# Sharing out a depthwise convolution anew, and beginning it during the projection ahead of it

## What is computed

```python
def conformer_conv(h, pw1_w, pw1_b, dw_w, dw_b, ln_g, ln_b, pw2_w, pw2_b):
    a = h @ pw1_w + pw1_b                      # first pointwise projection, 1024 -> 2048
    u, g = jnp.split(a, 2, axis=-1)
    u = u * jax.nn.sigmoid(g)
    u = lax.conv_general_dilated(u, dw_w[:, None, :], window_strides=(1,),
        padding=[(CONV_PAD, CONV_PAD)], dimension_numbers=("NWC", "WIO", "NWC"),
        feature_group_count=D_MODEL) + dw_b    # depthwise, 31 taps
    mu = jnp.mean(u, axis=-1, keepdims=True)
    var = jnp.mean(jnp.square(u - mu), axis=-1, keepdims=True)
    u = ((u - mu) * lax.rsqrt(var + NORM_EPS)) * ln_g + ln_b
    return jax.nn.silu(u) @ pw2_w + pw2_b      # second pointwise projection
```

## Time and profile before

| What | Value |
|---|---|
| Median of 3 runs | 3033.05 us (3025.01 to 3033.93) |
| The profiled execution's span, first to last instruction | 3031.5 us |
| Mean granted TensorE clock, as a share of full speed | 0.930 |
| TensorE matmul busy | 2768.4 us (91%) |
| VectorE busy | 1539.5 us (51%) |
| ScalarE busy | 1286.9 us (42%) |
| GpSimd busy | 142.2 us (5%) |

### The profile page before, as it was taken

The page is one execution under the profiler, slowest core; times in us unless marked ns, Lnnn a source line. Parts: engine busy times, 40 slices in busy tenths (PEclk is TensorE's granted clock), DMA queues, the critical chain, the costliest instruction groups (busy, mean ns, idle before and its releaser), DMA issues. The chain is left out here.

```text
span 3031.5 us, 41708 instructions
## 1 busy us (share of the span) xinstructions
PE 2768.4 (91%) x15680; PEld 2291.4 (76%) x15680; DVE 1539.5 (51%) x2209; ACT 1286.9 (42%) x1896; POOL 142.2 (5%) x114
## 2 busy tenths in 40 slices
PE   5999998995899999899998798997999988888997
PEld 3778786843678778678876658997769987867997
DVE  4544424397644433544323565546645456465554
ACT  4544422333444432444312354544435545354543
POOL 0000000750000000000000000000000001000000
PEclk9999999998999999999999899998869999679998
DMA  6344442200344433344322202543314444302543
GB/s 233 139 152 163 173 151 82 92 19 1 111 152 166 153 111 111 125 149 156 126 96 97 98 1 108 183 178 141 111 42 159 169 160 154 125 1 83 181 166 128
DMA packets 52713, 374.70 MB, mean 124 GB/s; under 512 B 5823, under 2 KB 7035, under 8 KB 8737
## 3 DMA queue, kind: packets, MB, share of 16 engines
q1 hardware_dynamic: 50144, 358.63, 33.0%
q0 software_dynamic: 1920, 12.27, 1.2%
q10 hardware_dynamic: 576, 2.83, 0.3%
HBM read 372.55 MB, written 7.39 MB: 125 GB/s over the span
## 5 line engine op out<-in xcount | busy, mean ns | idle before, releaser
L968 DVE TENSOR_TENSOR wlo<-raw,whi 128x1024 fp32r<-128x1024 f32 x682 | 823.0, 1229 | 921.7 <-ACT whi L631 921.3
L631 ACT ACTIVATE whi<-raw 128x1024 fp32r<-128x1024 f32 x682 | 701.0, 1053 | 923.9 <-PE acc L1378 855.7
L1376 PE MATMUL acc<-hhi,whi 128*128 128x256 f32 (+1 forms) x2768 | 933.5, 337 | 70.0 <-DVE hlo L1033 40.2
L1377 PE MATMUL acc<-hlo,whi 128*128 128x256 f32 (+1 forms) x2768 | 928.4, 335 | 0.0
L1378 PE MATMUL acc<-hhi,wlo 128*128 128x256 f32 (+1 forms) x2768 | 927.2, 335 | 0.0
L1376 PEld LDWEIGHTS acc<-hhi,whi 128*128 128x128 f32 x2768 | 535.0, 193 | 131.2 <-issue 78.6
L1378 PEld LDWEIGHTS acc<-hhi,wlo 128*128 128x128 f32 x2768 | 534.9, 193 | 50.8
L1377 PEld LDWEIGHTS acc<-hlo,whi 128*128 128x128 f32 x2768 | 535.2, 193 | 48.4 <-issue 0.2
L1376 PE MATMUL acc<-ghi,whi 128*128 128x512 f32 (+1 forms) x1056 | 363.4, 344 | 21.7 <-DVE glo L1079 21.7
L1377 PE MATMUL acc<-glo,whi 128*128 128x512 f32 (+1 forms) x1056 | 361.4, 342 | 0.0
L1378 PE MATMUL acc<-ghi,wlo 128*128 128x512 f32 (+1 forms) x1056 | 360.5, 341 | 0.0
(11 more groups left out here) (222 smaller groups left out, 2671.9 us busy)
## 6 DMA issues: line engine op xcount, KB each, us to landing
raw<-in_slabs SPq DMA_DIRECT2D x341, 1024.0 KB, 4.8
skew_dram<-lines_dram POOLq DMA_DIRECT2D x1, 6144.0 KB, 23.6
bt<-skew_dram POOLq DMA_DIRECT2D x4, 1024.0 KB, 6.9
x<-in_x_in ACTq DMA_DIRECT2D x1, 2048.0 KB, 8.1
out<-x SPq DMA_DIRECT2D x1, 1024.0 KB, 4.8
rope<-in_rope POOLq DMA_DIRECT2D x1, 512.0 KB, 4.7
mask<-in_mask POOLq DMA_DIRECT2D x1, 512.0 KB, 5.3
ptok<-in_p POOLq DMA_DIRECT2D x2, 256.0 KB, 5.2
```

Source lines behind the costliest of these rows:

```text
L631: nc.scalar.activation(whi[:, n % 2, cols], raw[:, n % 2, cols], ACT.Copy).then_inc(ready, 1)
L968: nc.vector.tensor_tensor(wlo[:, n % 2, cols], raw[:, n % 2, cols], whi[:, n % 2, cols].bitcast(F32), ALU.subtract).then_inc(low, 1)
L1376: nc.tensor.matmul(out, w[0], xx[0], start=first, stop=False)
L1377: nc.tensor.matmul(out, w[0], xx[1], start=False, stop=False)
```

## The change

The convolution's tiles are shared out as 0 and 1 (VectorE, early), 2 and 3 (GpSimd), 4 and 5 (VectorE, late), 6 and 7 (TensorE).
- Tap 0 with the bias is now made by ScalarE for tiles 0 to 5 (`first_tap`), each pair once its values are in `ubuf`.
- For tiles 2 and 3, ScalarE makes the products of taps 1 to 30 (`products`, 60 of them) into a ring of four buffers, and GpSimd only adds them to `v` (60 adds), the two tiles in turn.
- VectorE makes taps 1 to 30 of tiles 0 and 1 as one chain of 60 multiply-adds, of which 51 stand inside `pw1`, in portions of 9 and 8 between its casts; the other 9 and the 60 of tiles 4 and 5 follow in `conv`.
- ScalarE's products 0 to 27 stand inside `pw1`, in portions of 7, the rest beside the diagonals in `conv`. The diagonals of taps 0 and 1 are written ahead of the last cast of `pw1`.
- TensorE has two tiles in place of three for each tap. It sums tiles 0 and 1 first, then 6 and 7, 2 and 3, and 4 and 5 last.
- Two one-column activations (`preload`) stand ahead of the waits for the root and the SiLU.
- The loops of `pw1` and `conv` on ScalarE and of both on VectorE are written out instead of looped.

```diff
-POOL_TILES, DVE_TILES, PE_TILES = (0,), (1, 2, 3, 4), (5, 6, 7)
+DVE_EARLY, POOL_TILES, DVE_LATE, PE_TILES = (0, 1), (2, 3), (4, 5), (6, 7)
+CHAIN = 2 * (CONV_W - 1)
+RING = 4
...
+                pool.wait_ge(tap0_ready, 4)
+                for i in range(CHAIN):
+                    j = POOL_TILES[i % 2]
+                    pool.wait_ge(prod_ready, i + 1)
+                    if i >= 2:
+                        pool.wait_ge(conv_pool, i - 1)
+                    nc.gpsimd.tensor_tensor(v[:, j, :], v[:, j, :], tap_out[:, i % RING, :], ALU.add)\
+                        .then_inc(conv_pool, 1)
...
+            def first_tap(st, i):
+                act.wait_ge(acc_free[(st.m0 + 1) % 2], freed(st.m0 + 1) + i)
+                for j in (2 * i, 2 * i + 1):
+                    w, b = VCOL["dw_w"] + CONV_W * j, VCOL["dw_b"] + j
+                    nc.scalar.activation(v[:, j, :].rearrange("p (s t) -> p s t", s=2), ub2[:, 2 * j:2 * j + 2, 0:S],
+                                         ACT.Identity, bias=vec[:, b:b + 1], scale=vec[:, w:w + 1])\
+                        .then_inc(tap0_ready, 1)
+            def products(first, last):
+                for i in range(first, last):
+                    j, t = POOL_TILES[i % 2], 1 + i // 2
+                    w = VCOL["dw_w"] + CONV_W * j + t
+                    if i >= RING:
+                        act.wait_ge(conv_pool, i - RING + 1)
+                    nc.scalar.activation(tap_out[:, i % RING, :].rearrange("p (s t) -> p s t", s=2),
+                                         ub2[:, 2 * j:2 * j + 2, t:t + S], ACT.Copy, scale=vec[:, w:w + 1])\
+                        .then_inc(prod_ready, 1)
...
             def pw1(st):
-                with act.Fori(0, 4) as i:
+                for i in range(4):
+                    if i:
+                        first_tap(st, i - 1)
+                    if i >= 2:
+                        products(14 * i - 28, 14 * i - 21)
                     act.wait_ge(slab_used, st.n0 + 1 + 2 * i)
...
-                    hi(st.n0 + 2, i, 2)
-                    hi(st.n0 + 3, i, 2)
+                    hi(st.n0 + 2 + 2 * i)
+                    if i >= 2:
+                        products(14 * i - 21, 14 * i - 14)
+                    if i == 3:
+                        diagonals(0)
+                        diagonals(1)
+                    hi(st.n0 + 3 + 2 * i)
             def conv(st):
+                for t in range(CONV_W):
+                    if t >= 2:
+                        diagonals(t)
+                    products(28 + t, 29 + t)
+                products(28 + CONV_W, CHAIN)
...
+            def chain(first, last):
+                for i in range(first, last):
+                    late, at = divmod(i, CHAIN)
+                    j, t = (DVE_LATE if late else DVE_EARLY)[at % 2], 1 + at // 2
+                    w = VCOL["dw_w"] + CONV_W * j + t
+                    if at < 2:
+                        dve.wait_ge(tap0_ready, 6 if late else 2)
+                    if i >= 2:
+                        dve.wait_ge(conv_dve, i - 1)
+                    tile = v[:, j, :].rearrange("p (s t) -> p s t", s=2)
+                    nc.vector.scalar_tensor_tensor(tile, ub2[:, 2 * j:2 * j + 2, t:t + S], vec[:, w:w + 1], tile,
+                                                   ALU.mult, ALU.add).then_inc(conv_dve, 1)
             def pw1(st):
-                with dve.Fori(0, 4) as i:
-                    lo(st.n0 + 2, i, 2)
+                for i in range(4):
+                    if i:
+                        chain(17 * i - 17, 17 * i - 8)
+                    lo(st.n0 + 2 + 2 * i)
+                    if i:
+                        chain(17 * i - 8, 17 * i)
                     dve.wait_ge(acc_free[a], freed(st.m0) + i)
                     dve.wait_ge(slab_used, st.n0 + 2 + 2 * i)
...
-                    lo(st.n0 + 3, i, 2)
+                    lo(st.n0 + 3 + 2 * i)
             def conv(st):
...
+                chain(51, 2 * CHAIN)
                 dve.wait_ge(mean_done, 1)
...
+                pe.wait_ge(conv_dve, CHAIN)
+                for j in DVE_EARLY:
+                    mean_of(j, first=(j == 0))
                 pe.wait_ge(acc_free[0], 1 + (m + 1) // 2)
                 pe.wait_ge(acc_free[1], 1 + m // 2)
-                pe.wait_ge(conv_dve, len(DVE_TILES) * CONV_W)
-                pe.wait_ge(conv_pool, len(POOL_TILES) * (2 * CONV_W - 1))
-                for c in range(DT):
-                    ins = nc.tensor.matmul(B[2][:, :], ones, v[:, c, :], start=(c == 0), stop=(c == DT - 1))
+                for j in PE_TILES:
+                    mean_of(j)
+                pe.wait_ge(conv_pool, CHAIN)
+                for j in POOL_TILES:
+                    mean_of(j)
+                pe.wait_ge(conv_dve, 2 * CHAIN)
+                for j in DVE_LATE:
+                    ins = mean_of(j, last=(j == DVE_LATE[-1]))
```

More of the change, by code:

```diff
@@ L425, in build @@
         conv_pool = sem("conv_pool")
+        tap0_ready = sem("tap0_ready")
+        prod_ready = sem("prod_ready")
         mean_done = sem("mean_done")
@@ L631, in hi, with preload @@
                     nc.scalar.activation(whi[:, n % 2, cols], raw[:, n % 2, cols], ACT.Copy).then_inc(ready, 1)
+            spares = iter(range(32))
+            def preload(func):
+                at = next(spares)
+                nc.scalar.activation(spare[:, at:at + 1], eps[:, :], func)
             def start(st):
@@ L748, in conv @@
-            def conv(st):
-                def tap(t, par, wait):
-                    if wait is not None:
-                        act.wait_ge(taps_used, wait)
-                    for j in PE_TILES:
-                        ins = nc.scalar.activation(diag[:, par, j - PE_TILES[0], :], ident, ACT.Copy,
-                                                   scale=vec[:, bass.ds(VCOL["dw_w"] + CONV_W * j + t, 1)])
-                    ins.then_inc(diag_ready, 1)
-                tap(0, 0, None)
-                tap(1, 1, None)
-                with act.Fori(0, 14) as i:
-                    tap(2 * i + 2, 0, 2 * i + 1)
-                    tap(2 * i + 3, 1, 2 * i + 2)
-                tap(30, 0, 29)
-                act.wait_ge(taps_used, 31)
+                    hi(st.n0 + 2 + 2 * i)
@@ L1132, in pw1 @@
                     for t in range(2):
+                        at = VCOL["pw1_b"] + t + 2 * i
                         ins = nc.vector.scalar_tensor_tensor(
[L1134 to L1136 removed]
+                            ub2[:, 2 * t + 4 * i:2 * t + 4 * i + 2, PAD:PAD + S],
+                            acc[:, b, t, :].rearrange("p (s t) -> p s t", s=2), vec[:, at:at + 1],
                             gate_sb[:, t, :].rearrange("p (s t) -> p s t", s=2), ALU.add, ALU.mult)
                     ins.then_inc(acc_free[b], 1)
[L1139 removed]
+                    lo(st.n0 + 3 + 2 * i)
             def conv(st):
[L1143 to L1157 removed]
+                chain(51, 2 * CHAIN)
                 dve.wait_ge(mean_done, 1)
@@ L1540, in conv, with mean_of @@
                 tap(30, 0, 31, last=True)
+                def mean_of(c, first=False, last=False):
+                    return nc.tensor.matmul(B[2][:, :], ones, v[:, c, :], start=first, stop=last)
                 m = st.m0 + 2
+                pe.wait_ge(conv_dve, CHAIN)
+                for j in DVE_EARLY:
+                    mean_of(j, first=(j == 0))
                 pe.wait_ge(acc_free[0], 1 + (m + 1) // 2)
                 pe.wait_ge(acc_free[1], 1 + m // 2)
-                pe.wait_ge(conv_dve, len(DVE_TILES) * CONV_W)
-                pe.wait_ge(conv_pool, len(POOL_TILES) * (2 * CONV_W - 1))
-                for c in range(DT):
-                    ins = nc.tensor.matmul(B[2][:, :], ones, v[:, c, :], start=(c == 0), stop=(c == DT - 1))
+                for j in PE_TILES:
+                    mean_of(j)
[5 more added lines that the diff above has]
+                    ins = mean_of(j, last=(j == DVE_LATE[-1]))
                 ins.then_inc(mean_done, 1)
```

42 lines of the change are left out of this document (18 added, 24 removed).

## The result

The changed kernel takes 3042.18 us (median of 11 runs, 3035.69 to 3044.79), the kernel before 3030.14 us (11 runs, 3017.08 to 3033.93) beside it: ratio 1.0045, 95% interval 1.0034 to 1.0056. It is 12 us slower; 3027, and a gain of 6, was predicted.

A forecast was written before the change was run, and what follows sets the result against it. VectorE was taken to bound the kernel from 608 to 710, TensorE the projection ahead. Taps' end -2.8, fewer records behind them -5.1, squares' sum +2.0: -5.9 us, 3033.05 to 3027; own range 3018 to 3036 (0.62), with rivals 2996 to 3044.

The forecast's parts named there:

- An add's price: In the convolution, each GpSimd add beside VectorE's taps holds VectorE up 1.01 us; 60 adds cost 60.6 us.
- The schedule of the projection: VectorE's idle time in the projection is filled with taps; its fourth evacuation ends at about 628, not 608.
- Four records behind the last tap: Sum over the tiles: four records instead of 16 follow the last tap, 3.75 us against 8.87, so -5.1 us.
- The squares' sum behind them: Sum of squares after the mean begins at 1.2 GHz with three tiles late: +2 us, bounds 0 and +6.
- TensorE's taps behind 21.3 us of idle time: TensorE's convolution taps begin 20 us later, at about 628, and 62 matmuls take 53.3 us, to 682.
- cold taps: Rival: TensorE's convolution taps stay at half clock, 106.6 us, to 735; +23 us, 3056; chance 0.06.
- adds back to back alternate with VectorE: In the convolution, GpSimd waits only for VectorE's running operation, then holds the next: one operation per add, 1.01 us each.
- VectorE without idle time from 567 to 707: Sign that the forecast is right: VectorE works through from the projection to its last convolution tap.
- the last rival: Among other outcomes, an unseen wait between ScalarE, GpSimd and VectorE in one ring; no size given; chance 0.08.
- whole lock: Rival: each add holds VectorE its full 1.28 us, convolution taps end at 723; +10.4 us, 3043; chance 0.10.
- the end of the taps: VectorE's last convolution tap ends at 707 instead of 709.75: -2.8 us.

The follow-up runs named there:

- the bare stretches: Kernels without the convolution's code: stretches of 20 to 30 VectorE instructions, GpSimd operations let loose in each; back to back, 1.70 us per add.
- one pause: Changed kernel with one wait more, VectorE's 56th tap for GpSimd's 31st add: 3021.87 us beside 3023.81 for the kernel before, ratio 0.9992.
- the looser wait: Changed kernel with VectorE's taps 55 to 84 each waiting for an add four behind: 3029.96 us beside 3029.16 for the kernel before, ratio 0.9998.
- the versions with the loop: Changed kernel with VectorE's last 60 taps as a loop with register addresses again: 3050.68 us, ratio 1.0065 to the kernel before.
- swapped order: Changed kernel with ScalarE's product ahead of the two diagonals of the same tap in the second half: 3043.69 us, ratio 1.0048 to the kernel before.
- run 3042: The changed kernel itself, nothing further altered, against the kernel before: 3042.18 us beside 3030.14, ratio 1.0045.
- k = 6: Stretch of 30 VectorE multiply-adds without the forward pass, GpSimd's add released behind the first k finished instructions, here 6: the add takes 1.70 us.

## Why the prediction was wrong, point by point

**Held.** An add's price (predicted 1.01 us): in the bare stretches an operation of VectorE's was 1.00 us late and an add took 1.70; with one pause, 65 taps and 29 adds stand in 73.34 us, 1.04 per add. That the price is paid 60 times did not hold: 30 adds met no tap of VectorE's but waited or came behind it. The schedule of the projection: last evacuation at 630.15 + 1.40 = 631.55, less 1.5 of clock 630; predicted 628. Four records behind the last tap, 3.75 us: 3.78 with the looser wait, 3.61 with one pause. The squares' sum behind them, +2.0: 10.29 us in place of 7.71, +2.6, in the version with the looser wait, and 9.21, +1.5, with one pause. The number held, its reason isn't shown: it was that only 3.8 us of matmuls stand ahead, but the changed kernel's sum takes 9.62 with 51 us of matmuls ahead (granted clock 0.50 over its first 1.7 us), and 7.98 in the versions with the loop and with the swapped order, in which TensorE does the same. TensorE's taps behind 21.3 us of idle time: with one pause they have a granted clock of 0.52 over the first 5 us and 1.00 from then on, take 55.88 us in place of 53.3 and end at 688.72, less 2.67 of clock 686; predicted 682. The rival "cold taps" had them at half clock throughout and fell.

**Failed.** The step is this sentence: "From there I take that adds back to back alternate with VectorE, one of its operations for each: GpSimd waits for the running one and then holds the next." Adds back to back do. But behind the projection the adds don't come back to back: ScalarE makes a product only each 1.72 us, and behind the 30th add GpSimd idles 8.47 us for the next one, which ScalarE makes only behind diagonals that wait for TensorE, and TensorE for the last evacuation. The 31st add came into a VectorE that by then had had nothing of GpSimd's between for two taps, two evacuations, two casts and over four taps more, and it was kept out for 43.8 us. In the sum this is the wait of an add for VectorE's stream, put at nothing beyond the running operation. The prediction named "VectorE without idle time from 567 to 707" as a sign that it is right, and never asked what an unbroken stream does to an engine that comes late to it. From there the chain is the one that the last rival named without a size, "an unseen wait between ScalarE, GpSimd and VectorE in one ring, 0.08": GpSimd holds ScalarE's buffers, ScalarE's queue holds TensorE's diagonals.

Its size, on a common clock: TensorE's last tap ends at 726.3 - 1.5 = 724.8, 42.8 behind the predicted 682, 7 more than its one wait: its taps begin 2 us later than predicted and take 58.7 us in place of 53.3, a part of them behind the wait at a granted clock of 0.50; and with it gone as the end, all 16 records of the mean follow it, so that the mean comes at 733.21 - 1.5 = 731.7 in place of the forecast 710.75. That VectorE ends at 679.5 - 1.5 = 678, 29 us before the forecast, buys nothing.

**The result's number near "whole lock" is chance.** That rival gave 3043; the run 3042. Its mechanism, 1.28 us per add, is not there: an add cost 1.00 to 1.04, and VectorE's taps end 29 us before the forecast, not 16 behind it.

**The forecast's size, with the failed step mended.** One pause: on the common clock (545.55 against 542.88 for the casts of slab n0+3, 2.67 late) the mean is ready 716.41 - 718.90 - 2.67 = -5.2 us, where the forecast had -2.8 - 5.1 = -7.9, and the wait takes 1.73 of the difference. By the reciprocal behind the squares (728.70 against 729.60) it is -3.6 in the stage, against -5.9. The sum was right to 2.3 us. By its terms: the end of the taps +0.3 (712.72 - 709.75 - 2.67) where it had -2.8, with the wait in it; the records of the mean -5.5 where it had -5.1; from the mean to the reciprocal +1.6 where it had +2.0. Whether the whole program would gain from it isn't shown: the ratio with one pause has 1 in its interval.

**Cause and what is not shown.** That the kept-out add costs the time is shown: three versions that keep the changed kernel's work and differ in a wait of VectorE's lose all of the slowdown, and three that leave the add kept out (loop, swapped order, the change itself) are slower by 0.45 to 0.65%. Why the border is at seven instructions, and how an evacuation enters the count, is not.

## What to carry to other kernels

Where VectorE runs operations with SBUF inputs without a break, ask of every GpSimd operation not how long it takes but when it comes: one that follows closely on the last costs each side a known turn, one that comes late into a long stream can wait for its end, and takes along whatever shares a ring with it. Look in the tile view at the longest duration beside the median (43825 beside 1703 ns here); a mean hides it. And if each turn of GpSimd's takes more from VectorE (1.0 us) than VectorE would need for the work itself (0.66), take the work off GpSimd.

## What the runs showed of the hardware

- GpSimd adds against VectorE's SBUF-to-SBUF operations: a 512-column add holds VectorE up for 1.0 us of its 1.27, a one-input multiply of the same size for 0.43. In the bare stretches a stream of one kind of VectorE operations without a pause lets a GpSimd add in only if it comes within its first seven (six, for 1024-column casts): 1.70 us at k = 6, 16.28 at k = 7. From then on the add waits until the stream ends, in the changed kernel 43.8 us, over the last 64 of 69 multiply-adds. A pause of VectorE's or a turn of GpSimd's starts the count anew. Streams of nothing but evacuations out of PSUM or memsets neither keep it out nor are held up (adds of 1.27 us at k = 5 to 12).
- The Trainium skill (SBUF — State Buffer, section "SBUF: two separate sides") has the shared port pair go to whichever starts first, for the whole instruction, and only against VectorE operations with two SBUF inputs or in a two-port mode. The traces agree that evacuations (one input from PSUM) are out of it, at 1.27 us per add beside them. They differ in two things: VectorE is held for 1.0 us, not for the add's whole 1.27, and an add that comes behind the first seven does not get the pair at the end of the running instruction, but of the running stream (16.28 us in the stretch with k = 7).
- TensorE's granted clock, a mean of its two levels, 1.2 and 2.4 GHz: 0.64 of full speed over 631 to 679.5, in which it has 14.57 us of matmuls and then stands, and 0.92 over 679.5 to 727, with matmuls from 682 on.
```profile
631.00:679.50 48.50, 14.57 (x28) 6.12 (x28) 48.50 (x72) 5.92 (x14) 42.67 (x1) 0.64 0.06 22
679.50:727.00 47.50, 44.87 (x99) 19.54 (x99) 0.04 (x1) 33.18 (x76) 37.54 (x30) 0.92 0.00 0
```
The columns are those of the earlier trace rows; the first also holds the 42.67 us of the one add on POOL.
